# Turning the convolution histories later, and a wider last output turn, in a two-layer decoder step

## The reference

```python
h = rmsnorm(x, l0_norm_mix_pre)
gate_b, gate_c, u, q, k, v = split(h @ l0_w_in)          # the first projection, 24 tiles of 128 columns
conv_out, new_hist = causal_dwconv(gate_c * u, state_conv_a, l0_conv_w)   # needs the old rows (histories)
y_b = attend(q, k, v)                                     # samples read pages of cache_k, cache_v
...
xbc, new_conv_hist = causal_dwconv(xbc, state_conv_ssm, l1_conv_w)        # layer 1, the other histories
...
x = x + rmsnorm(ffn(x), l1_norm_ffn_post)                 # the last addition; x is y_prompt and y_sample
```

## Time and profile before

| | us |
|---|---|
| median of 3 runs | 1107.51 (1104.77 to 1107.94) |
| the profiled execution | 1100.03 |
| its span, first to last instruction | 1098.0 |
| PE busy in the span | 1027.7 (94%) |
| DVE busy | 706.6 (64%) |
| ACT busy | 502.9 (46%) |
| mean granted clock of TensorE | 0.963 of 2.4 GHz |

### The profile page before, as it was taken

One profiled execution on the slowest core, in us unless ns is written; L12 is line 12 of the kernel. 1 busy time (PEld: TensorE's weight loads), 2 busy tenths in 40 slices (PEclk: granted clock), 3 DMA queues, 4 the chain that ended last, 5 costly groups with the idle time before them and its releaser, 6 DMA issues.

```text
span 1098.0 us, 21757 instructions
## 1 busy us (share of the span) xinstructions
PE 1027.7 (94%) x8763; PEld 941.6 (86%) x8763; DVE 706.6 (64%) x1303; ACT 502.9 (46%) x901; POOL 54.0 (5%) x97
## 2 busy tenths in 40 slices
PE   8799999879889999999889999899999799999996
PEld 7799888533479999999879999777889699999994
DVE  5454668655549666643498997788974775665343
ACT  5131444232455344343458675564764543444341
POOL 8000400000000000000000000021000000000000
PEclk9899999979998999999989999899999899999998
DMA  9474999999973455455524555089035255544501
GB/s 303 127 250 152 285 349 348 340 345 347 346 221 115 156 176 169 147 165 164 178 78 153 166 180 154 1 276 360 21 124 159 87 177 162 182 155 145 173 30 43
DMA packets 193074, 206.17 MB, mean 188 GB/s; under 512 B 7172, under 2 KB 185561, under 8 KB 192923
## 3 DMA queue, kind: packets, MB, share of 16 engines
q1 hardware_dynamic: 174046, 178.65, 51.6%
q10 hardware_dynamic: 15232, 14.68, 4.2%
q0 software_dynamic: 3696, 11.45, 3.3%
HBM read 192.59 MB, written 12.17 MB: 186 GB/s over the span
## 4 chain that ended last, share of the span: by engine, by line
PE 81%; DVE 8%; DMA 3%; POOL 2%; ACT 2%; SPq 2%; issue 1%; ACTq 0%; POOLq 0%; DVEq 0%
PE acc L815 20%; PE acc L817 20%; PE acc L816 20%; PE trb L908 3%; PE scb L929 3%; PE acc L908 3%; PE scb L1041 2%; SPq L590 2%; PE scb L786 1%; DVE RR L1792 1%; DVE X L2201 1%; DVE Y L2200 1%; DMA ring<-in_state_ssm_dram 1%; DVE WHL L1815 1%; DMA out_dram<-ring 1%
## 5 line engine op out<-in xcount | busy, mean ns | idle before, releaser
L815 PE MATMUL acc<-HX,WHL 128*128 128x288 f32 x928 | 278.6, 300 | 14.8 <-DVE HX L1804 10.9
L816 PE MATMUL acc<-HX,WHL 128*128 128x288 f32 x928 | 275.3, 297 | 0.0
L817 PE MATMUL acc<-HX,WHL 128*128 128x288 f32 x928 | 274.7, 296 | 0.0
L1394 ACT ACTIVATE WHL<-ring 128x1024 fp32r<-128x1024 f32 (+1 forms) x140 | 138.8, 1039 | 192.6 <-PE acc L817 192.6
L1815 DVE TENSOR_TENSOR WHL<-ring,WHL 128x1024 fp32r<-128x1024 f32 (+1 forms) x140 | 163.4, 1207 | 71.6 <-ACT WHL L1394 71.6
L815 PEld LDWEIGHTS acc<-HX,WHL 128*128 128x128 f32 x928 | 176.0, 190 | 18.3 <-issue 13.7
L816 PEld LDWEIGHTS acc<-HX,WHL 128*128 128x128 f32 x928 | 177.6, 191 | 0.2
L817 PEld LDWEIGHTS acc<-HX,WHL 128*128 128x128 f32 x928 | 177.3, 191 | 0.0
L1394 ACT ACTIVATE W<-ring 128x1024 fp32r<-128x1024 f32 x84 | 82.6, 1032 | 130.4 <-PE acc L817 130.4
L1815 DVE TENSOR_TENSOR W<-ring,W 128x1024 fp32r<-128x1024 f32 x84 | 97.1, 1196 | 54.1 <-ACT W L1394 54.0
L815 PE MATMUL acc<-HX,W 128*128 128x288 f32 x352 | 105.3, 299 | 6.2 <-DVE HX L1804 5.8
(11 more groups left out here) (407 smaller groups left out, 1858.7 us busy)
## 6 DMA issues: line engine op xcount, KB each, us to landing
ring<-in_l_w_in_dram SPq DMA_DIRECT2D x32, 1024.0 KB, 5.4
ring<-in_l_ffn_gate_dram SPq DMA_DIRECT2D x22, 1024.0 KB, 5.4
ring<-in_l_ffn_up_dram SPq DMA_DIRECT2D x22, 1024.0 KB, 5.3
ring<-in_l_ffn_down_dram SPq DMA_DIRECT2D x16, 1024.0 KB, 5.2
Z<-in_cache_k_dram SPq DMA_DIRECT2D x52, 256.0 KB, 6.8
ring<-in_cache_k_dram SPq DMA_DIRECT2D x52, 256.0 KB, 6.8
Z<-in_cache_v_dram SPq DMA_DIRECT2D x48, 256.0 KB, 7.0
ring<-in_cache_v_dram SPq DMA_DIRECT2D x48, 256.0 KB, 6.1
```

The source lines that it names most:

```text
L815: pe.matmul(out, w[:, 0, at:at + P], part_at(k, 0), start=(k == 0), stop=False)
L816: pe.matmul(out, w[:, 0, at:at + P], part_at(k, 1), start=False, stop=False)
L817: last = pe.matmul(out, w[:, 1, at:at + P], part_at(k, 0), start=False, stop=(k == kdim - 1))
L1394: act.activation(split_weights(i)[:, 0, half], ring[:, slot_of(u), half], ACT.Copy).then_inc(w_hi, 1)
```

## The change

It moves `turn_histories` from behind pair 1 to behind pair 7 (the eighth), and with it ACT's and DVE's copies; ACT's wait for `ld_head` and the cast of `wdt` move there too. At the end DVE adds in two blocks of four tiles. PE turns the first halves of all three t, then the second halves, each into a bank of its own (the four `acc` banks and two `trb`), after a wait until all `acc` banks are free. ACT copies the three first halves and the second half of t = 1, DVE the second halves of t = 0 and t = 2, under new semaphores.

```diff
+    HIST_POS = 7
...
+        Y_BANKS = (acc[0], acc[1], acc[2], acc[3], trb[0], trb[1])
...
             for t in range(3):
-                sp.wait_ge(tr_act, (TR_Y + 2 * t + 2) // 2)
-                sp.wait_ge(tr_dve, (TR_Y + 2 * t + 2) // 2)
+                sp.wait_ge(y_first, t + 1)
+                sp.wait_ge(*((y_dve, t // 2 + 1) if t % 2 == 0 else (y_act, 1)))
...
             def after_first(pair):
-                if pair == 1:
+                if pair == HIST_POS:
                     turn_histories()
...
             pe.wait_ge(ring_read, G * RING_STEPS)
-            for t in range(3):
-                rows = P if t < 2 else NS
-                for i in range(2):
-                    bank = tr_open(TR_Y + 2 * t + i)
+            pe.wait_ge(acc_free, n_acc[0])
+            for i in range(2):
+                pe.wait_ge(x_made, 3 * KD + 4 * i + 4)
+                for t in range(3):
+                    rows = P if t < 2 else NS
                     for c in range(4):
-                        k = 4 * i + c
-                        pe.wait_ge(x_made, 3 * KD + k + 1)
-                        last = pe.transpose(bank[0:rows, c * P:(c + 1) * P], X[:, k, t * P:t * P + rows], ident[:, :])
-                    last.then_inc(tr_full, 1)
+                        last = pe.transpose(Y_BANKS[3 * i + t][0:rows, c * P:(c + 1) * P], X[:, 4 * i + c, t * P:t * P + rows], ident[:, :])
+                    last.then_inc(y_turned, 1)
...
             root(D)
-            act.wait_ge(ld_head, 64)
-            act.activation(WDT_HI, wdt[:, :, :], ACT.Copy).then_inc(wdt_hi, 1)
             for i in range(N_OUT0):
                 if i:
                     next_split(i)
-                if i == 1:
+                if i == HIST_POS:
+                    act.wait_ge(ld_head, 64)
+                    act.activation(WDT_HI, wdt[:, :, :], ACT.Copy).then_inc(wdt_hi, 1)
                     copy_transposed(TR_HIST, hista[:, :, :, :], ...
...
             for t in range(3):
                 rows = P if t < 2 else NS
-                copy_transposed(TR_Y + 2 * t, YT[0:rows, t, 0:4 * P], trb[0][0:rows, :])
+                act.wait_ge(y_turned, t + 1)
+                act.activation(YT[0:rows, t, 0:4 * P], Y_BANKS[t][0:rows, :], ACT.Copy).then_inc(y_first, 1)
+            act.wait_ge(y_turned, 5)
+            act.activation(YT[:, 1, 4 * P:8 * P], Y_BANKS[4][:, :], ACT.Copy).then_inc(y_act, 1)
...
-                if i == 3:
+                if i == 2 * HIST_POS + 1:
                     third = CC // 3
...
-                for size in (1, 1, 2, 2, 2):
+                for size in (1, 1, 2, 2, 2) if hx is not None else (4, 4):
...
-            for t in range(3):
+            for t in (0, 2):
                 rows = P if t < 2 else NS
-                copy_transposed(TR_Y + 2 * t + 1, YT[0:rows, t, 4 * P:8 * P], trb[1][0:rows, :])
+                dve.wait_ge(y_turned, 4 + t)
+                dve.tensor_copy(YT[0:rows, t, 4 * P:8 * P], Y_BANKS[3 + t][0:rows, :]).then_inc(y_dve, 1)
```

More of the change, by code:

```diff
@@ L394, in hybrid_decoder_kernel @@
         kv_stored = sem("kv_stored")
+        y_turned = sem("y_turned")
+        y_first = sem("y_first")
+        y_act = sem("y_act")
+        y_dve = sem("y_dve")
         y_stored = sem("y_stored")
```

## The result

The changed kernel takes 1099.55 us (median of 5, 1099.05 to 1102.84), the kernel before 1107.49 in the same measurement (5 runs, 1104.77 to 1107.94). The ratio of the two is 0.9944, 95% interval 0.9924 to 0.9965: 3.9 to 8.4 us faster, 6.2 by the ratio itself; the medians differ by 7.94. The forecast was 1099.5, a gain of 8.0 us.

A forecast was written before the change was run, and what follows sets the result against it. TensorE carried 81% of the chain of waits, so only its standing still or lower clock counted. Start 11.5 - 4.6 = 6.9 us plus end 1.1 gave 8.0, taken from the median 1107.51: 1099.5 us, range 1094.0 to 1104.0.

The forecast's parts named there:

- Gap removed, 10.15 us: First projection: TensorE starts the third pair at 30.03 instead of 40.18, 10.15 us earlier.
- Slow third pair, 1.4: Third pair's first twelve matmuls: at full clock they take 1.58 us instead of 2.96, 1.4 us back.
- Stall behind the eighth pair, 4.6: Moved histories stop TensorE between pairs 8 and 9 for 4.36 to 4.85 us, taken as 4.6.
- the two idle pieces foretold: Within the stall behind pair 8: about 1.3 us before the third bank, at most 0.7 before the fourth.
- "I take 0" for the clock in the moved histories: Behind pair 8: the clock stays full, costing 0; 1.4 us kept for the range.
- rival 1: Clock falls in the moved histories, pair 9 starts at 1.2 GHz: gain 6.6 us, 1100.9; chance 0.24.
- Key loads hidden: SP's queue: key loads begin at about 73.9 instead of 66.18, but the later start costs nothing.
- The slack: SP's queue: free at 102.5, third sample's first key load due at 105.7, 3.2 us to spare.
- the start: First projection: 11.5 us removed less 4.6 us added, net gain 6.9 us.
- The end, 1.1: Final additions, transposes, copies and stores: span ends 1.1 us earlier, bounds 0.5 and 2.0.
- the stores' own time: Final three stores: issued nearly back to back, their data time takes most of the copies' 2.0 us gain, leaving 1.1.
- The sum: Whole kernel: 6.9 at the start plus 1.1 at the end, 8.0 us, giving 1099.5.

The follow-up runs named there:

- The tenth pair's run: Changed kernel with the histories behind the tenth pair instead of the eighth: 1107.18 us against 1107.64 of the kernel before, ratio 1.0000 (0.9982 to 1.0018).
- the two places tried between them: Histories behind the eighth pair (changed kernel, 1099.55 us, ratio 0.9944) or behind the fourth (1100.58 us, ratio 0.9935), each against the kernel before.

## Why the prediction was right, and where it was not

**Gap removed, 10.15 us.** Right for the profile that was read: 10.09. The third pair waits 0.3 us for a PSUM bank, as foretold. The other profiles with the old start show a gap that is 1.3 us longer, since the history load landed later.

**Slow third pair, 1.4.** 1.27 in that profile, 2.1 and 2.8 in the two others.

**Stall behind the eighth pair, 4.6.** 4.65 measured, with the two idle pieces foretold (1.72 and 0.62 against 1.3 and 0.7).

**"I take 0" for the clock in the moved histories.** This step failed, and rival 1 is what happened, in all three profiles of the new start, at 1.5 to 2.85 us where 1.4 was allowed. The argument compared the stall with two stretches from 105 and 205 us that kept 1.00. The nearer row was the kernel's own: the same transposes with the same kind of waits had been followed by 0.50 from 40.2 to 43. There the clock had fallen even earlier, while PE stood still for the history load (stretches and PE's timeline of before):

```profile
30.00:32.00 2.00, 0.00 (x0) 0.00 (x0) 1.86 (x3) 0.00 (x0) 0.00 (x0) 1.00 0.46 88
32.00:34.00 2.00, 0.26 (x3) 0.27 (x3) 0.00 (x0) 0.00 (x0) 0.00 (x0) 0.70 0.80 226
33.74 0.60 PE L870 MATMUL trb<-ident,Z 16*128 16x16 f32 x4 [3.91 <-DMA Z<-in_state_conv_ssm_dram]
```

And the comparison itself doesn't hold from one execution to the next: in the changed kernel's profile the K and V turns, moved forward to 100.4, had 0.54 from 105.2 to 108, in its second profile 1.00.

**Key loads hidden.** Right: third sample's first load at 109.04, SP idle before it. The slack was 6.1 us (109.04 less 101.73 and 1.2 for page numbers), not 3.2, since that load came due 3.3 us later than forecast: the start gave 5.05 us and not 6.9; the fallen clock in the K and V turns cost 1.1 us (8.82 instead of 7.74 from the projection's last matmul to that load); and the executions' first 26 us differ by 0.4. That second fall is seen in three of the ten profiles with later histories and in none of the four with the old start; whether the change brings it stays open. The tenth pair's run shows the price once the slack is gone.

**The end, 1.1.** 1.14 in the profiles that were read, and by the cause named, the stores' own time: counted from the last reciprocal, the last copy ends 2.05 us earlier (2.0 forecast), the first store is issued 0.42 earlier (0.5 forecast). With all output transposes at 0.50 in both it is 1.5.

**The sum.** By the terms of the first pair of profiles the change is worth 5.05 + 1.14 = 6.2 us, not 8.0 (5.1 with the loss in the K and V turns); by the means of all profiles above, 6.2 + 1.6 = 7.8. The ratios say 6.2 (3.9 to 8.4) and, measured again, 4.5 (2.5 to 6.4). So that the median came out at 1099.55 is partly luck: the clock's loss of some 2 us was missed, and an old gap about 1.3 us longer than in the profiled execution, with a slower third pair, made up for part of it. How much lies between 4.5 and 7.8 us the runs don't settle.

## What to carry to other kernels

Work that waits for late data belongs behind the point where the data have landed, and before the point where something queued behind it is due; both points can be read from the profile, and the two places tried between them gave the same time. The waits inside the moved work are worth as much again: with as many PSUM banks as fills, the same step at the same place cost 1.96 us instead of 4.65 and left the clock alone, 4.2 us better in the trace. An earlier last copy pays until the last transfers run back to back; from there on only an earlier first byte does.

## What had not been expected of the hardware

The clock in the same work differs from run to run. From 260 to 310 us, with the DMA engines full, the granted clock was 0.97 in the first profile of before, 0.86 in that of after, 0.76 in the second of before, and 0.76 to 0.93 in the others. A single profile's span is therefore worth little for a change of 6 us: the two spans first compared here differ by 0.3, and the second profile of before took 1109.02 us where the first took 1100.03.
